# One merged stage of 32 units for the differential attention, its keys zero-padded to 128 rows

## What is computed

```python
qkv = h @ w_qkv                                   # 1024 -> 3 x 1024, 8 heads
q = rms_norm_2(qkv[..., :qk_w].reshape(b, s, 8, 2, 64), q_gain)      # two maps of 64 per head
k = rms_norm_2(qkv[..., qk_w:2 * qk_w].reshape(b, s, 8, 2, 64), k_gain)
v = qkv[..., 2 * qk_w:].reshape(b, s, 8, 128)
# for each block of 128 queries:
    sc = jnp.einsum('bqhcd,bkhcd->bhcqk', q_blk, k) * 64 ** -0.5 + bias      # causal
    a = jax.nn.softmax(sc, axis=-1)
    wts = a[:, :, 0] - lam * a[:, :, 1]
    o = jnp.einsum('bhqk,bkhv->bqhv', wts, v)
o = rms_norm_2(o, sub_gain) * (1.0 - lam_init)
h = h + o.reshape(b, s, 1024) @ w_o
```

## Time and profile before

| | us |
|---|---|
| median of three executions | 3387.99 |
| the profiled execution | 3379.43 |
| its span (first to last instruction) | 3377.5 |
| TensorE busy in the span | 3072.3 |
| VectorE / ScalarE / GpSimd busy | 1399.3 / 937.3 / 1292.2 |
| first dense matmul of `DiffHeads` to the end of the last one of `a_w_o` | 1598.4 to 1979.1 |

### The profile page before, as it was taken

The page is one execution under the profiler, slowest core; times in us unless marked ns, Lnnn a source line. Parts: engine busy times, 40 slices in busy tenths (PEclk is TensorE's granted clock), DMA queues, the critical chain, the costliest instruction groups (busy, mean ns, idle before and its releaser), DMA issues.

```text
span 3377.5 us, 38890 instructions
## 1 busy us (share of the span) xinstructions
PE 3072.3 (91%) x12698; PEld 2278.2 (67%) x12698; DVE 1399.3 (41%) x2309; ACT 937.3 (28%) x1617; POOL 1292.2 (38%) x631
## 2 busy tenths in 40 slices
PE   6999989886798999987888889999779999899998
PEld 2688856663486688865555568887546677688886
DVE  6211243883234311245322355542643544455425
ACT  3211022333312211023333323320334552233202
POOL 0455443220154555444222245554441112455544
PEclk9999989898999999998878899999889999999999
DMA  4222321110032222321111122232211111222232
GB/s 160 74 93 92 92 72 57 50 62 19 13 106 87 65 95 93 92 72 62 53 53 54 40 88 98 92 90 84 83 56 42 38 32 51 80 93 93 89 92 94
DMA packets 78588, 249.14 MB, mean 74 GB/s; under 512 B 9072, under 2 KB 15728, under 8 KB 78384
## 3 DMA queue, kind: packets, MB, share of 16 engines
q1 hardware_dynamic: 64800, 229.74, 21.1%
q10 hardware_dynamic: 13712, 18.44, 1.7%
HBM read 238.57 MB, written 9.44 MB: 73 GB/s over the span
## 4 chain that ended last, share of the span: by engine, by line
PE 83%; DVE 8%; ACT 4%; issue 2%; POOL 1%; DMA 1%; ACTq 0%; DVEq 0%; POOLq 0%; SPq 0%
PE ps L297 23%; PE ps L298 23%; PE ps L299 23%; DVE tmp L493 2%; PE ps L1926 2%; PE ps L1895 1%; PE ps L2210 1%; PE ps L2251 1%; PE ps L2229 1%; PE ps L2230 1%; PE ps L1293 1%; PE ps L1116 1%; POOL xl L481 1%; PE ps L452 1%; PE ps L1868 1%
## 5 line engine op out<-in xcount | busy, mean ns | idle before, releaser
L291 POOL TENSOR_TENSOR w_lo<-raw,w_hi 128x1024 fp32r<-128x1024 f32 (+1 forms) x438 | 1038.9, 2372 | 1463.3 <-DVE w_hi L284 1463.3
L297 PE MATMUL ps<-xh,w_hi 128*128 128x512 f32 x2248 | 912.5, 406 | 59.2 <-DVE xl L481 34.3
L298 PE MATMUL ps<-xl,w_hi 128*128 128x512 f32 x2248 | 895.1, 398 | 0.0
L299 PE MATMUL ps<-xh,w_lo 128*128 128x512 f32 x2248 | 894.5, 398 | 0.0
L284 DVE CAST w_hi<-raw 128x1024 fp32r<-128x1024 f32 (+1 forms) x438 | 330.1, 754 | 1338.3 <-PE ps L299 1319.5
L297 PEld LDWEIGHTS ps<-xh,w_hi 128*128 128x128 f32 x2248 | 425.4, 189 | 202.4 <-issue 52.6
L298 PEld LDWEIGHTS ps<-xl,w_hi 128*128 128x128 f32 x2248 | 426.8, 190 | 104.0 <-issue 4.8
L299 PEld LDWEIGHTS ps<-xh,w_lo 128*128 128x128 f32 x2248 | 425.9, 189 | 104.7
L297 PE MATMUL ps<-ah,w_hi 128*128 128x512 f32 x704 | 278.1, 395 | 0.0
L298 PE MATMUL ps<-al,w_hi 128*128 128x512 f32 x704 | 278.1, 395 | 0.0
L299 PE MATMUL ps<-ah,w_lo 128*128 128x512 f32 x704 | 278.1, 395 | 0.0
(11 more groups left out here) (360 smaller groups left out, 3722.1 us busy)
## 6 DMA issues: line engine op xcount, KB each, us to landing
raw<-in_ffn_up SPq DMA_DIRECT2D x90, 512.0 KB, 3.5
raw<-in_conv_up SPq DMA_DIRECT2D x88, 512.0 KB, 3.5
raw<-in_ffn_down SPq DMA_DIRECT2D x32, 512.0 KB, 3.5
raw<-in_conv_down SPq DMA_DIRECT2D x32, 512.0 KB, 3.5
raw<-in_merge SPq DMA_DIRECT2D x24, 512.0 KB, 3.6
raw<-in_ple_gate SPq DMA_DIRECT2D x24, 512.0 KB, 4.4
raw<-in_diff SPq DMA_DIRECT2D x24, 512.0 KB, 3.5
raw<-in_mla SPq DMA_DIRECT2D x20, 512.0 KB, 3.5
```

The costliest lines, as they stand in the source:

```text
L291: pool.tensor_tensor(self.w_lo[s][:, 0:n], self.raw[r][:, 0:n], self.w_hi[s][:, 0:n].bitcast(F32), ALU.subtract).then_inc(self.sem["slot_s ...
L297: pe.matmul(out, wh, xh, start=start, stop=False)
L298: pe.matmul(out, wh, xl, start=False, stop=False)
L299: return pe.matmul(out, wl, xh, start=False, stop=stop)
```

## The change

`DiffHeads` and its `OutProj` are replaced by `Diff` and `DiffOut`. All values are projected first (`value_rows`): x is the stationary operand and the weights stream, so V comes out in token rows and needs no transposes. Each x tile serves 12 dense matmuls before the next is needed. Then 32 units run in one stream, with half of a Q or K projection of a later head in 26 of them. Logits have one bank per map. `dk` is 128 rows per map, the other map's 64 rows hold zeros (two memsets at the start), and the K norm writes each half by an instruction of its own. The last units and the stage's end have tiles of the output projection among them, in a hand-written order (`ORDER`, `BESIDE`).

```diff
-class DiffHeads(Stage):
-    ROUNDS = HEADS // 2
+class Diff(Stage):
+    UNITS = 4 * HEADS
+    V_BANKS = ((3, 4, 5, 6), (0, 1, 2, 7))
+    def item_in(self, u):
+        h, b = u // 4, u % 4
+        item = ("K", h + 1) if b < 2 else ("Q", h + 2)
+        return (item, b % 2) if item[1] < HEADS else (None, 0)
+    def sums_in(self, u):
+        h, b = u // 4, u % 4
+        key = {0: ("Q", h + 1), 2: ("K", h + 1), 3: ("O", h - 1)}.get(b)
+        return [key] if key is not None and 0 <= key[1] < HEADS else []
+    def value_rows(self, pe, g):
...
+            for t in range(2):
+                x = 2 * part + t
+                if g == 0:
+                    pe.wait_ge(*self.x_ready(x))
+                for tb in range(NB):
+                    pe.matmul(out, k.xh[:, x, own], wh, start=x == 0, stop=False)
+                    pe.matmul(out, k.xh[:, x, own], wl, start=False, stop=False)
+                    mm = pe.matmul(out, k.xl[:, x, own], wh, start=False, stop=x == KD - 1)
+    def logits(self, pe, u):
...
+        for c in range(2):
+            if u:
+                pe.wait_ge(*self.on("row_min", 2 * u - 2 + c))
-                        pe.matmul(bank[:, 0:P * (b + 1)], k.dq[64 * c:64 * c + 64, j, b * P:(b + 1) * P],
-                                  k.dk[64 * c:64 * c + 64, j, 0:P * (b + 1)], start=True, stop=False)
+            pe.matmul(k.ps[:, c, 0:n], k.dq[:, h % 2, b * P:n], k.dk[:, h % 2, c, 0:n], start=True, stop=False)
+            pe.matmul(k.ps[:, c, b * P:n], k.ident_b, k.causal_b, start=False, stop=True
+                      ).then_inc(k.sem["logits"], 1)
+    def values(self, pe, u):
...
+        for s in range(b + 1):
+            mm = pe.matmul(k.ps[:, 3 + h % 2, b * P:(b + 1) * P], k.dvr[:, s, h * P:(h + 1) * P],
+                           k.dpt[:, u % 2, s * P:(s + 1) * P], start=s == 0, stop=s == b)
     def tensor(self, pe):
+        self.value_rows(pe, 0)
+        self.value_rows(pe, 1)
+        self.project(pe, ("Q", 0), 0)
...
+        for u in range(self.UNITS):
+            self.logits(pe, u)
+            for key in self.sums_in(u):
+                self.sum_squares(pe, key)
+            item, half = self.item_in(u)
+            if item is not None:
+                self.project(pe, item, half)
+            self.out.beside(pe, u)
+            if u >= 2:
+                self.turn(pe, u - 2)
+            if u >= 3:
+                self.values(pe, u - 3)
     def scalar(self, act):
+        self.biases(act, 0)
+        self.biases(act, 1)
...
+            self.exp(act, u)
+            if b == 3 and h + 2 < HEADS:
+                self.biases(act, h + 2)
     def norm_out(self, dve, key):
...
+            for c in range(2):
+                own = slice(64 * c, 64 * c + 64)
+                ins = dve.scalar_tensor_tensor(k.dk[own, h % 2, c, :], self.bank(key)[own], k.vecs[own, gain:gain + 1],
+                                               k.tmp[2 + n % 2][own, :], ALU.mult, ALU.mult)
     def vector(self, dve):
+        dve.memset(k.dk[64:P, :, 0, :], 0.0).then_inc(k.sem["key_zero"], 1)
+        dve.memset(k.dk[0:64, :, 1, :], 0.0).then_inc(k.sem["key_zero"], 1)
+        for pos in range(self.VALUES + 1):
+            k.round_hi(dve, self.w, 0, pos + 2)
...
+class DiffOut(Stage):
+    BANKS = (5, 6, 3, 0, 1, 5, 6, 3)
+    EARLY = [(m, t) for m in range(2) for t in range(5)] + [(0, 5), (1, 5)]
+    OPEN = [(m, t) for m in (3, 4, 2) for t in range(6)]
+    ORDER = (EARLY + OPEN + [(m, t) for t in (6, 7) for m in range(5)] + [(m, t) for m in (5, 6, 7) for t in range(KD)])
+    BESIDE = {26: (0, 3), 27: (3, 6), 28: (6, 8), 29: (8, 10), 30: (10, 12)}
...
     def vector(self, dve):
+        heads.combine(dve, Diff.UNITS - 1)
+        heads.output_lo(dve, 6)
...
+        for m in range(KD):
+            dve.wait_ge(*self.done(m))
+            dve.tensor_tensor(k.h[:, m, :], self.bank(m), k.h[:, m, :], ALU.add).then_inc(k.sem["added"], 1)
+            if m == 0:
+                k.round_hi(dve, self.w, 0, 6)
+            if m >= 5:
+                k.round_hi(dve, self.w, 0, m + 2)
+            dve.wait_ge(*self.on("squared", m))
+            if m:
+                dve.wait_ge(*self.on("acc_sum", m - 1))
+            dve.tensor_tensor(k.acc[:], k.acc[:], k.sq[m % 2][:], ALU.add).then_inc(k.sem["acc_sum"], 1)
-    heads = add(DiffHeads(k, add(PreNorm(k, V["attn_norm0"], after=h))))
-    h = add(OutProj(k, "a_w_o", k.oh, k.ol, HEADS, after=heads))
+    heads = add(Diff(k, add(PreNorm(k, V["attn_norm0"], after=h))))
+    h = add(DiffOut(k, heads))
```

More of the change, by code:

```diff
@@ new lines, in scalar @@
+        self.biases(act, 1)
+        for g in range(2):
+            for tb in range(NB):
+                self.value_out(act, g, tb)
+        self.square(act, ("Q", 0))
+        self.rstd(act, ("Q", 0))
+        self.square(act, ("K", 0))
+        self.rstd(act, ("K", 0))
+        self.square(act, ("Q", 1))
+        for u in range(self.UNITS):
+            h, b = u // 4, u % 4
+            self.exp(act, u)
+            if b == 3 and h + 2 < HEADS:
+                self.biases(act, h + 2)
+            for key in self.sums_in(u):
+                self.rstd(act, key)
+            item, half = self.item_in(u)
+            if item is not None and half == 1:
+                self.square(act, item)
+            if b == 0 and h >= 2:
+                self.output_hi(act, h - 2)
+            if u >= 2:
+                self.turned_out(act, u - 2)
+            if b == 2 and h >= 1:
+                self.square(act, ("O", h - 1))
@@ new lines, in row_min @@
+    def row_min(self, dve, u):
+        k, h, b = self.k, u // 4, u % 4
+        if b == 0:
+            dve.wait_ge(k.dma[f"tile_in{h % 2}"], self.tile_base[h % 2] + 64 * (h // 2 + 1))
+        for c in range(2):
+            m, i = 2 * u + c, (2 * u + c) % 16
+            dve.wait_ge(*self.on("logits", m))
+            if u >= 2:
+                dve.wait_ge(*self.on("probs", u - 2))
+            k.carry(dve)
+            dve.tensor_tensor_reduce(k.de[:, m % 4, 0:P * (b + 1)], k.ps[:, c, 0:P * (b + 1)],
+                                     k.dbias[:, h % 2, TRI[b]:TRI[b + 1]], -1.0, 3e38, ALU.add, ALU.min,
+                                     k.small[:, i:i + 1]).then_inc(k.sem["row_min"], 1)
@@ new lines, in combine @@
+    def combine(self, dve, u):
+        k, width, i = self.k, P * (u % 4 + 1), 2 * u % 16
+        first, second = k.de[:, 2 * u % 4, 0:width], k.de[:, 2 * u % 4 + 1, 0:width]
+        dve.wait_ge(*self.on("probs_raw", 2 * u + 1))
+        dve.reciprocal(k.small[:, 32 + i:34 + i], k.small[:, 16 + i:18 + i]).then_inc(k.sem["row_recip"], 1)
+        dve.wait_ge(*self.on("row_recip", u))
+        if u >= 2:
+            dve.wait_ge(*self.on("probs_t", u - 2))
+        w = k.dw[:, u % 2, 0:width]
+        dve.tensor_scalar(w, second, k.small[:, 33 + i:34 + i], k.neg_lam[:], ALU.mult, ALU.mult
+                          ).then_inc(k.sem["scaled"], 1)
+        dve.wait_ge(*self.on("scaled", u))
+        dve.scalar_tensor_tensor(w, first, k.small[:, 32 + i:33 + i], w, ALU.mult, ALU.add
+                                 ).then_inc(k.sem["probs"], 1)
@@ new lines, in output_lo @@
+    def output_lo(self, dve, h):
+        k = self.k
+        dve.wait_ge(*self.on("y_hi", h))
+        dve.tensor_tensor(k.ol[:, h, :], k.dout[:, h % 2, :], k.oh[:, h, :].bitcast(F32), ALU.subtract
+                          ).then_inc(k.sem["y_lo"], 1)
+    def vector(self, dve):
+        k = self.k
+        dve.memset(k.dk[64:P, :, 0, :], 0.0).then_inc(k.sem["key_zero"], 1)
+        dve.memset(k.dk[0:64, :, 1, :], 0.0).then_inc(k.sem["key_zero"], 1)
+        for pos in range(self.VALUES + 1):
+            k.round_hi(dve, self.w, 0, pos + 2)
+        self.norm_out(dve, ("Q", 0))
+        k.round_hi(dve, self.w, 0, self.VALUES + 3)
+        self.norm_out(dve, ("K", 0))
+        k.round_hi(dve, self.w, 0, self.VALUES + 4)
+        for u in range(self.UNITS):
+            h, b = u // 4, u % 4
+            self.row_min(dve, u)
+            if u >= 1:
+                self.combine(dve, u - 1)
+            for key in self.sums_in(u):
+                self.norm_out(dve, key)
+            if b == 1 and h >= 2:
+                self.output_lo(dve, h - 2)
+            item, half = self.item_in(u)
+            if item is not None and half == 1:
+                k.round_hi(dve, self.w, 0, self.slot(item) + 2)
+            self.out.split_beside(dve, u)
```

471 lines of the change are left out of this document (255 added, 216 removed).

## The result

The changed kernel takes 3283.6 us (median of four, 3281.6 to 3284.9) against 3388.8 before; the ratio is 0.969, with a 95% interval from 0.9676 to 0.9705. The prediction was 3290, with a range from 3277 to 3322. The two kernels were measured side by side three times: 3283.6, 3284.4 and 3286.0 against 3388.8, 3384.8 and 3385.9.

The account below looks back on a forecast made before the run. TensorE was taken as the bound, at a mean clock of 0.84. Its work of 265.2 us plus small terms made a stage of 282.2 against 380.7, 98 us less: 3388 - 98 = 3290 us, range 3277 to 3322.

Parts of the forecast that it names:

- TensorE's work at full clock, 265.2 us: New stage: dense matmuls, logits with masks, transposes, values and sums of squares, priced by distances between starts, sum to 265.2 us.
- Clock 1.00 in the units: Windows of the new stage's units: full clock, with TensorE over 19 busy of 20 us.
- A stream made of 64-row matmuls: Old stage's units: 64-row logits took the clock though TensorE was busy; the low clock cost 56 us.
- So idle gaps are not what took the clock: Old stage's units: the clock fell with TensorE busy for 2.00 of 2.00 us, so gaps did not start it.
- The trace shows only the second: Old logits: the trace shows mode changes draining the engine, not row tiles in parallel; maps start 1.21 us apart.
- weight tile 2: Stage start: two memsets stand on DVE ahead of this tile's rounding and hold TensorE for 0.5 us.
- units 28 to 31 and the last `combine`: Last units, with few or no dense matmuls: 3 us of idle time, and 0.5 behind the last combine.
- the stall: `DiffOut`: TensorE waits 5 us for the rounding of the last weight tile, behind tile 5's add and POOL's low half.
- the later last sum: Stage end: the last running sum waits for POOL's low half some 0.6 us longer than before.
- The clock in stretches: Rival, units: the clock falls in stretches, giving 3314 us for six units or 3342 for more; chance 0.14.
- the paced units: Rival: VectorE or ScalarE paces the units; one microsecond in each of 32 gives 3322 us; chance 0.10.
- the slower one: Rival: half-empty-array matmuls lose the clock, so the units' 162 us take twice as long, 3452 us; chance 0.03.

Follow-up runs that it names:

- e2: The kernel before with one part of the change, keys padded to 128 rows per map, rounds, banks and order kept: 3358.9 us.
- e11: The kernel before with both maps' 64-row logits directly behind one another in each unit, then both masks: 3352.3 us.
- e1: The changed kernel with each map's logits reading only their own 64 rows of queries and keys: 3296.9 us.
- e3: The changed kernel with two more VectorE memsets in each of the 32 units, filling buffers that nothing reads: 3285.1 us.

## Why the prediction held, and where its steps did not

- **TensorE's work at full clock, 265.2 us.** Right within 2%. The stage took 283.4 us to its last matmul's end (1883.17), against 281.6 predicted for it. Without the waits and the low clock that the trace shows (13.5 us, below), 269.9 are left, 4.7 more than priced: logits with masks took 40.9 instead of 38.2, since the second map of a unit takes 0.97 and not 0.92, dense matmuls and sums of squares some 3 more than 200.4. The added terms came out 2.9 smaller than their 16.4, so that the stage was met better than its parts; that much was luck. Pricing from `Mla`'s starts carried the forecast.
- **Clock 1.00 in the units.** Right, all slices.
- **The cause of the low clock before.** "A stream made of 64-row matmuls" was half right. e2 confirms it in the first round, where the clock fell with TensorE busy (and rose at 1666.8, not 1666.4); e11 shows that 64-row matmuls in pairs keep it. "So idle gaps are not what took the clock" was read from the first round alone: in the second the low clock began behind the gap of 2.3 us ahead of the units, and did not end in the 64-row logits, where e2 kept the full clock. The price was nearly right: summed over the stage's matmuls the low clock cost 53 us, against 56 predicted.
- **What the padding is worth.** The prediction gave no price for each part, but its closing sum put 19 us on the form and 56 on the clock, as if rows were the key to both. Of the 100 us the merged stage without the padding brings 88 (e1), and it brings the clock with it. The padding adds 12.5 in the medians and 16.8 in the profiled stages. There TensorE is busy for 17.8 us less than in e1, 1.7 of them the low clock behind the wait in e1's last units, and idle for 1.0 more. What the merged stage's own parts bring (V first and without transposes, the units in one stream, the output tiles among them, `ol` on VectorE) was not run apart.
- **"The trace shows only the second."** Wrong as a reading of parallel work. The mask of 128 rows stood between the two maps in every row, so no row could show it. The time of the changed kernel was not touched by this, but the better version was missed: pairs instead of padding.
- **Small terms.** Low clock at the start 1.5, measured about 1.6 (eight matmuls 0.43 apart); weight tile 2 0.5, measured 1.2; first logits 0.7, measured 0.4; units 0 to 27 2.8, measured 1.3; units 28 to 31 and the last `combine` 3.5, measured 2.2, all of it in one wait behind unit 31; add of tile 5 0.9, measured 1.3; the stall 5, measured 3.7, because a cycle of add, square and sum took 2.0 us, not 2.3; the clock behind it 1.5, measured about 1.8; the later last sum 0.6, measured 1.5 (10.5 us from the last matmul's start to the next stage's first, 9.0 before).
- **Rivals.** The clock in stretches, the paced units and the slower one did not come. e3 rules out VectorE in the second, with a microsecond a unit to spare, and the trace's waits ScalarE.

The median came out 6 us below the forecast. The trace explains none of it: the profiled execution took 3284.9, 4 us more than the 3281 predicted for it. It is the offset between median and profiled execution, 8.6 us in the kernel before, which the prediction took over to the kernel after, where it is about -1. The two errors partly cancel.

## What to carry to other kernels

Price a merged stream from a stage that already runs one: the distance between starts at full clock, kind by kind, plus each wait that can be named. Before speeding up the engine that looks like the bound, ask what the others' chain takes in the same unit: the same padding took 42 us off TensorE's busy time in the split stage and gave 26. The merged stage gave three times as much even with the slower 64-row logits: it has other work beside that chain, TensorE's idle time went from 36.9 to 9.0 us and the clock from 0.84 to 0.98 (e1). A row that cannot show an effect, because of what stands between, is no evidence against it.

## What was not expected of the hardware

Two float32 matmuls of 64 rows each, on partitions 0 to 63 and 64 to 127 and into two PSUM banks, ran in the time of one (1.06 us at 512 columns) when issued in a row. A map of 512 columns between 128-row matmuls takes 1.21 us from start to start and 0.92 to 0.97 when padded, which makes 0.12 to 0.15 us for each of its two changes of form; so pairs were worth it from 256 columns on (0.82 against 1.01 for the pair with its masks). And in the first round's units the clock was granted in full to such pairs with TensorE busy for 0.8 to 1.6 of 2 us, while single 64-row matmuls lost it at 2.00 of 2.
